# Where the sixty-four pieces of the copy of V stand on the SyncE queue, in a decoder-layer kernel on one NeuronCore

## What is computed

```python
proj = jnp.einsum('bld,de->ble', xn, w_in)          # one input projection, cut into q/k/v, gates, selectors
# mixer A: causal conv, gated delta rule (chunks, triangular solve), per-head norm, gate
# mixer B: rotary, retention with per-head decay, per-head norm, gate
merged = (jax.nn.sigmoid(sel_a) * jnp.einsum('blv,vd->bld', o_a, w_br_a)
          + jax.nn.sigmoid(sel_b) * jnp.einsum('blv,vd->bld', o_b, w_br_b))
return jnp.einsum('bld,de->ble', merged, w_out), conv_new, s_delta_new, s_ret_new
# then PEER: top-16 of 128 x 128 experts for 8 heads
act = jax.nn.gelu(jnp.einsum('td,thkd->thk', xb, u_tab[eidx]).astype(jnp.float32), approximate=False)
coef = (gate * act).astype(xb.dtype)
return jnp.einsum('thk,thkd->td', coef, v_tab[eidx])
```

## Time and profile before

| | us |
|---|---|
| median of three runs | 2153.03 (2151.24 to 2167.64) |
| the profiled execution | 2147.17 |
| its span, first to last instruction | 2145.1 |
| mean granted TensorE clock | 0.97 of 2.4 GHz |

### The profile page before, as it was taken

One profiled execution on the slowest core, in us unless ns is written; L12 is line 12 of the kernel. 1 busy time (PEld: TensorE's weight loads), 2 busy tenths in 40 slices (PEclk: granted clock), 3 DMA queues, 4 the chain that ended last, 5 costly groups with the idle time before them and its releaser, 6 DMA issues.

```text
span 2145.1 us, 29753 instructions
## 1 busy us (share of the span) xinstructions
PE 1934.8 (90%) x10912; PEld 1566.1 (73%) x10912; DVE 1359.0 (63%) x2860; ACT 616.7 (29%) x1217; POOL 677.5 (32%) x556
## 2 busy tenths in 40 slices
PE   5998889977997888999999999999899998999886
PEld 4997889976976888999999999998543333434332
DVE  3219263343336344488899889998478777876663
ACT  4223312242224324344554445444300000000000
POOL 0003012100000000223333333232277776776663
PEclk9999899987998999999999999999999999999999
DMA  3727258839403854699999999999599999999997
GB/s 117 235 79 232 59 182 259 259 104 314 147 10 135 299 176 144 234 344 386 401 391 389 371 379 384 388 379 382 199 411 411 394 409 411 397 400 415 407 414 289
DMA packets 244650, 629.25 MB, mean 293 GB/s; under 512 B 19714, under 2 KB 137541, under 8 KB 226712
## 3 DMA queue, kind: packets, MB, share of 16 engines
q0 software_dynamic: 74880, 377.52, 44.2%
q1 hardware_dynamic: 169632, 249.92, 34.1%
HBM read 584.36 MB, written 110.21 MB: 324 GB/s over the span
## 4 chain that ended last, share of the span: by engine, by line
PE 22%; DMA 18%; DVE 11%; issue 4%; POOL 4%; ACT 2%; SPq 0%; DVEq 0%; POOLq 0%; ACTq 0%
DMA ex_uv_row<-value_rows,ex_eidx 12%; PE ps L2131 8%; DMA ex_w_raw<-in_peer_ut 6%; PE ps L584 4%; PE ps L586 4%; PE ps L585 4%; POOL ex_uv_row L2060 4%; DVE ex_fin L2382 3%; DVE ex_w_lo L1929 2%; DVE ex_uv_row L2370 1%; ACT ex_w_hi L2193 1%; DMA ex_w_raw<-in_peer_wq 1%; DVE ex_sel L2339 0%; DVE ex_sel L2343 0%; DVE ex_best L2342 0%
## 5 line engine op out<-in xcount | busy, mean ns | idle before, releaser
L2131 PE MATMUL ps<-ex_uv_row,ex_q_s 128*128 128x512 f32 (+1 forms) x1208 | 542.1, 599 | 61.3 <-DVE ex_q_s L2395 60.6
L2131 PEld LDWEIGHTS ps<-ex_uv_row,ex_q_s 128*128 128x128 f32 (+1 forms) x1208 | 217.2, 188 | 366.2 <-issue 332.6
L2060 POOL DMA_INDIRECT ex_uv_row<-value_rows,ex_eidx x384 | 407.5, 1061 | 212.3 <-PE ps L2131 116.2
L584 PE MATMUL ps<-x_hi,ex_w_lo 128*128 128x384 f32 (+2 forms) x1296 | 426.3, 329 | 18.0 <-DVE ex_w_lo L1929 13.4
L586 PE MATMUL ps<-x_hi,ex_w_hi 128*128 128x384 f32 (+2 forms) x1296 | 423.3, 327 | 0.0
L585 PE MATMUL ps<-x_lo,ex_w_hi 128*128 128x384 f32 (+2 forms) x1296 | 423.2, 327 | 0.0
L2044 POOL DMA_INDIRECT ex_uv_row<-in_peer_uv,ex_eidx x128 | 190.3, 1487 | 398.6 <-DVE ex_fin L2382 393.0
L2382 DVE SCALAR_TENSOR_TENSOR ex_fin<-ex_uv_row,ret_tables,ex_fin 128x1024 f32<-128x1024 f32 x218 | 278.9, 1280 | 0.3
L584 PEld LDWEIGHTS ps<-x_hi,ex_w_lo 128*128 128x128 f32 x1296 | 244.2, 188 | 28.4 <-DVE ex_w_lo L1929 17.9
L586 PEld LDWEIGHTS ps<-x_hi,ex_w_hi 128*128 128x128 f32 x1296 | 244.5, 189 | 0.0
L585 PEld LDWEIGHTS ps<-x_lo,ex_w_hi 128*128 128x128 f32 x1296 | 244.1, 188 | 0.0
(11 more groups left out here) (415 smaller groups left out, 3425.7 us busy)
## 6 DMA issues: line engine op xcount, KB each, us to landing
value_rows<-in_peer_uv SPq DMA_DIRECT2D x64, 1024.0 KB
ex_w_raw<-in_peer_ut SPq DMA_DIRECT2D x128, 512.0 KB, 8.7
value_rows<-ex_z_rows SPq DMA_DIRECT2D x128, 128.0 KB
first_raw<-in_w_in SPq DMA_DIRECT2D x8, 1024.0 KB, 8.4
ex_w_raw<-in_peer_wq SPq DMA_DIRECT2D x16, 512.0 KB, 9.3
value_rows<-ex_z_rows SPq DMA_DIRECT2D x128, 64.0 KB
dp_w_raw<-in_w_in SPq DMA_DIRECT2D x14, 512.0 KB, 4.3
ex_uv_row<-value_rows,ex_eidx POOLq DMA_INDIRECT x384, 10.2
```

Of the source, the lines that this page charges most:

```text
L584: pe.matmul(out, left(llo, c), right(rhi, c), start=(c == 0), stop=False)
L2060: pool.indirect_dma_start(value_slot(p)[0], None, k.value_rows, bass.IndirectOffsetOnAxis(ap=eidx[:, u, n % TOPK:n % TOPK + 1], axis=0), e ...
L2131: ins = pe.matmul(k.pv[j % 2][0:r, c, :], spread[:, on_tensor[p] % SPREADS, 0:r], v[:, c * 512:(c + 1) * 512], start=first, stop=last)
```

## The change

The table of first pieces gets other numbers, and a second and third table say behind which chunks' loads pieces stand (`COPY_CHUNKS`, one each) and how many follow once the last load of the stream is issued (`COPY_BEHIND`). No piece stands in the opening of a stream any more. `COPIES_BESIDE` gets a second number: how many of the tiles have pieces.

Pieces after: proj_a 6 behind the loads of chunks 2 to 7 and 6 after them; cv 6, for the first 6 of 8 tiles; dp 24, for the first 12 of 14; proj_b 4 behind the loads of chunks 4 to 7 and 7 after them; branches 4 behind the loads of chunks 4 to 7; w_out none beside loads and 7 after them. That is 12 + 6 + 24 + 11 + 4 + 7 = 64. The other engines' instructions are the same.

```diff
--- before.py
+++ after.py
@@ -80,10 +80,12 @@
 VECTOR_LAST = 1
 COPIES = 64
 COPY = NE // COPIES
-COPY_FROM = {"proj_a": 0, "cv": 8, "dp": 16, "proj_b": 44, "branches": 52, "w_out": 60}
+COPY_FROM = {"proj_a": 0, "cv": 12, "dp": 18, "proj_b": 42, "branches": 53, "w_out": 57}
+COPY_CHUNKS = {"proj_a": (2, 8), "proj_b": (4, 8), "branches": (4, 8)}
+COPY_BEHIND = {"proj_a": 6, "proj_b": 7, "w_out": 7}
 SIDE = 2 * H + 2 * DC
 SIDE_BESIDE = {"ba": 2, "cv": 8, "dp": 14}
-COPIES_BESIDE = {"cv": 1, "dp": 2}
+COPIES_BESIDE = {"cv": (1, 6), "dp": (2, 12)}
 FAR = -1e30
 LOWEST = -3.0e38
 
@@ -381,6 +383,7 @@
         products, taken, dve_own = (k.sem(f"{name}_{n}") for n in ("products", "taken", "dve_own"))
         FREE_RAW, FREE_PS, FREE_W = 2, 2, 2 * NT
         part = lambda n: slice(n * jobs[0].kc // PARTS, (n + 1) * jobs[0].kc // PARTS)
+        copy_from, copy_chunks = COPY_FROM.get(name, 0), COPY_CHUNKS.get(name, (0, 0))
 
         def plan():
 
@@ -424,12 +427,14 @@
                             for n, ((dst, src), done) in enumerate(zip(extra, extra_done)):
                                 if n not in late:
                                     sp.dma_start(dst, src).then_inc(done, 16)
-                            k.copy_values(sp, COPY_FROM[name])
-                        k.copy_values(sp, COPY_FROM[name] + chunk0 + 2 * i + b)
+                        elif copy_chunks[0] <= chunk0 + 2 * (0 if chunk0 else 1) and chunk0 < copy_chunks[1]:
+                            k.copy_values(sp, copy_from + chunk0 - copy_chunks[0] + 2 * i + b)
                     chunks(sp, job, chunk0, load)
                     if job is jobs[0]:
                         for n in late:
                             sp.dma_start(*extra[n]).then_inc(extra_done[n], 16)
+                for n in range(COPY_BEHIND.get(name, 0)):
+                    k.copy_values(sp, copy_from + copy_chunks[1] - copy_chunks[0] + n)
                 if then is not None:
                     sp.wait_ge(w_lo_done, FREE_RAW + 2 * sum(job.steps for job in jobs) - 1)
                     sp.dma_start(raw[0][:, :, :], then).then_inc(then_loaded, 16)
@@ -597,7 +602,7 @@
         before = sum(list(SIDE_BESIDE.values())[:list(SIDE_BESIDE).index(name)])
         self.tiles = range(before, before + SIDE_BESIDE[name])
         self.halves, self.quarter = 2 * SIDE_BESIDE[name], 0
-        self.copies, self.copy_from = COPIES_BESIDE.get(name, 0), COPY_FROM.get(name, 0)
+        (self.copies, self.copy_loads), self.copy_from = COPIES_BESIDE.get(name, (0, 0)), COPY_FROM.get(name, 0)
         self.k, (self.w, self.hi, self.lo, self.dram) = k, k.side_operands
         two = range(2)
         sb = lambda n, s, dt=F32: [k.sb(f"{name}_{n}{b}", s, dt, ctx) for b in two]
@@ -624,7 +629,8 @@
         for n, tile in enumerate(self.tiles):
             self.load(sp, n + 2)
             for piece in range(self.copies * n, self.copies * (n + 1)):
-                self.k.copy_values(sp, self.copy_from + piece)
+                if n < self.copy_loads:
+                    self.k.copy_values(sp, self.copy_from + piece)
             sp.wait_ge(self.taken, 2 * n + 2)
             sp.dma_start(self.dram[:, tile:tile + 1, :], self.result[n % 2][:, :, :]).then_inc(self.stored[n % 2], 16)
         for b in range(2 if self.halves else 0):
```

## The result

The changed kernel takes 2140.03 us, the median of 19 runs (2131.29 to 2151.95), beside 2157.22 of the kernel before (19 runs, 2145.17 to 2175.11). The ratio is 0.9918, with a 95% interval of 0.9896 to 0.994: 17.7 us less by the ratio, 17.2 by the two medians. Two later series gave 0.9901 (0.9862 to 0.994) and 0.9916 (0.9887 to 0.9946). Forecast were 18.5 us and 2134.5 us.

What follows compares the result with a forecast made beforehand. TensorE, busy 90% of the span, was taken as the bound, with time lost where it or a phase's end waits for SyncE's queue. Terms of 8.7, 6.3 and 3.5 us sum to 18.5: 2153.03 to 2134.5 us, range 2126 to 2145.

Steps and rivals of the forecast that it cites:

- The two waits and the phase's end: TensorE's waits of 7.8 us in proj_b and 6.6 in branches, and 5.50 us idle at the end of delta_solve.
- proj_b, 8.7 us: Opening of proj_b: chunk 2's load lands earlier, 7.3 us of TensorE's wait go, and 1.4 for the clock.
- The wait that stays: In proj_b's opening, 0.5 us of TensorE's 7.8 us wait at chunk 2 was to remain.
- the lower end: In proj_b, chunk 2's load is issued only at 520.08 and lands at 523.5; 4.4 us gained.
- the rival: Stages' own inputs hold the loads, SyncE held at the load as at pieces: gain 10.3 us, 2142.7; chance 0.15.
- branches, 6.3 us: Opening of branches: ScalarE's 4.4 us wait for chunk 4's load goes, and 1.9 us for the clock.
- The 2.2 us that no load is at fault for: In branches at chunk 4, 2.2 us of TensorE's wait stay: two splits don't fit into half a short chunk.
- End of the solve, 3.5 us: End of delta_solve: the last store finds an empty queue, 2.7 us, and 0.8 for the clock.
- The store's 2.7 us: At delta_solve's end the last store lands after 2.2 us, at 434.0 instead of 436.8: 2.7 us gained.
- Half of 1.6 for the clock: After delta_solve's end the clock's fall was worth up to 1.6 us; half, 0.8, was taken.
- The bursts, nothing: Pieces behind the last loads of proj_a, proj_b and w_out fit under the stage's remaining time: no cost.
- The price of 3.1 us a piece: From proj_b's end: each piece costs the DMA engines 3.1 us, so eight are 25 us of 45.

Runs made afterwards that it cites:

- r3: Kernel before with only proj_b's pieces moved out of its opening, behind later loads and the last load; 0.9937 of before, 2148.24 us.
- r5: Kernel before with only the last four pieces of delta_solve moved, behind the last load of w_out; 0.999 of before.
- r4: Kernel before with only branches' pieces moved, four behind loads of chunks 4 to 7, four behind w_out's last load; 0.9977 of before, 2154.13 us.
- r2: The changed kernel again, unchanged, with a second profile; 0.9901 of the kernel before.
- r9: The changed kernel again, unchanged, with a third profile; 0.9916 of the kernel before, median 2140.49 us.
- r6: Changed kernel with 19 instead of 7 pieces behind proj_b's last load, and one per tile in delta_solve instead of two; 0.9973 of before, 2153.97 us.
- r8: Changed kernel with S_sample behind chunk 3's load, sel_a's first two tiles sent ahead and ScalarE waiting for these alone; 0.9911 of before, 2133.27 us.
- r7: Changed kernel with S_sample behind chunk 3's load and sel_a's first two tiles sent ahead, ScalarE still waiting for the rest; 0.9908 of before, 2140.35 us.
- r10: The kernel of r8 again, timed beside the changed kernel; 0.9896 of the kernel before, median 2138.11 us.

## Why the prediction was right

*The bound.* The two waits and the phase's end that the timelines named were where the time came from. r3 to r5 show each by itself, in the lengths of the stages and the waits; that together they make the whole is shown within the intervals.

*proj_b, 8.7 us.* By the first pair of profiles 7.7, by all with and without the pieces 8.6: (126.8, 128.9, 127.3, 127.7) in the mean 127.7, beside 119.0 (119.1, 119.0, 118.9, 119.1). The wait that stays was forecast at 0.5 us and is 0.7 to 1.3. The clock kept to 1.00, as assumed. The step on which the lower end hung was put to the test by the kernel itself: SyncE was held at the load for 15.64 us, as the rival had it, and the load still landed 3.0 us behind S_sample (2.7 forecast). What counts is the place in the queue.

*branches, 6.3 us.* Measured 6.5 to 6.7 in r4, r2 and r9, 4.2 in the first profile, and 3.7 in r6, where sel_a landed later. The 2.2 us that no load is at fault for are there, 2.08. What the prediction didn't see is chunk 1: it took the clock to be safe up to chunk 4. In the first profile it rose early in chunk 0, TensorE came to ScalarE's wait for sel_a sooner, stood for 3.95 us instead of 2.27, and paid 4 us at half the clock. That isn't the change's doing: r3 and r5, with branches' pieces as before, have it too (gaps of 3.85 and 3.72 us at chunk 1), and there the stage is no longer for it, at 89.6 us, since it had chunk 4's load to wait for anyway.

*End of the solve, 3.5 us.* The store's 2.7 us are 2.4 to 3.0: the store was there 1.7 us after SyncE began to wait, some 2.0 after its issue. The fit in the Trainium skill (the page "DMA: Bandwidth & Descriptors", section "Anatomy of one DMA — SWDGE (gpsimd) path"), about 2.0 us and the bytes by 436 GB/s, gives an estimate of 3.2 us for this store. The row of this kernel's own stores, 2.2 us, was the better guide. Half of 1.6 for the clock was a coin's value: with the gap at 2.7 us delta_finish took 54.2 us in four profiles (after, r6, r8, r9) and 55.6 to 57.1 in four (r2, r5, r7, r10). With the longer gap it was 55.6 to 56.5 in all four. delta_solve alone differs by 4 us between profiles, so that its part shows only in the mean: 182.2 us in the four with pieces at its end, 179.6 in the eight without; with delta_finish, 238.2 and 234.7.

*The bursts, nothing.* Right for 7 and 8 pieces. The price of 3.1 us a piece was mis-sized; by the time that SyncE is held it is 3.6 for each further one. The 3.1 was half of the 6.3 us that one load and one piece kept the DMA engines busy, as if both cost the same, but at the prediction's own 391 GB/s the load is only 2.7 of them. That would not have changed the term, but it moves the point from which a burst costs something. SyncE is free 11.5 us after it begins on eight, and 3.6 later for each one more, so the 46 us from the start of the burst to the stage's end would hold 17 pieces. That is an estimate from the runs with 8 and 20; no run has 17.

*The sum.* 18.5 us were forecast, 17.7 measured (12.9 to 22.4 by the interval). That the two are so near is in part luck: in the mean of the profiles of the two kernels the phases up to experts are 18.5 us shorter, but 16.5 of that lie in the stages of the three terms (8.8 in proj_b, 5.9 in branches, 1.8 in delta_solve and delta_finish) and 2.0 in others. The absolute time was 5.5 us over the forecast, 4.2 of it because the three runs shown before had a median of 2153.03, where more runs gave 2157.22.

*What the prediction had wrong* is a check that it set for itself. "An experts phase whose length, some 1303 us from 842 to the end, moves by more than 3 us" was to count against it. It moved by 13.7 us with no step at work; two executions of the kernel before differ in it by 5.6 us, three of the changed kernel by up to 13.6. A bound on a phase has to come from two profiles of the same kernel.

## What to carry to other kernels

Bulk traffic that nobody waits for soon belongs behind the last load of a stage, where its cover is the rest of the stage's computation; in a stage's opening, and ahead of the last store that a barrier waits for, it can show up as a wait, even where that wait is put down to another engine. It did in proj_b and branches, whose loads stood behind it; in proj_a and w_out, where TensorE waited for no load, it hadn't. The cover has an end, at the issuing engine: count the pieces by the time that they hold it, and see that it comes to the barrier in time. Judge a change of some 1% by the lengths of the phases that it touches, in more than one profile, and by many runs; the difference of two spans was 4 us here where the change was worth 17.7.

## What the runs showed that I had not expected

The experts phase takes between 1303.3 and 1323.4 us for the same instructions. From the first gather out of `value_rows` on it is the same 606 us within 1.3; the difference lies ahead of that, in the 650 to 670 us in which 512 KiB loads and indirect gathers share the DMA engines.

An early rise of the clock can make a stage longer. In branches' opening it gave 85.4 us in the one profile of the changed kernel that has it, the late rise gave 82.8 and 82.9: what the faster chunk 0 saved was idled away at a wait that was there already, and after that longer gap (3.95 us beside 2.3) the clock was at 0.50. A late rise with as long a gap is no better: in r6 sel_a landed later, the gap was 3.76 us, the clock fell behind it, and the stage took 85.8.

A gap of 2.7 us at the end of the solve cost the clock in four profiles of eight, one of 5.1 us or more in all four.
